# Modulation rows from transposed weights: VectorE multiplies by the conditioning row and sums along it

## The reference, cut to what matters

```python
def adaln(c, w, b):
    mod = jax.nn.silu(c) @ w + b                  # [1, 1024] @ [1024, 3072]
    shift, scale, gate = jnp.split(mod[:, None, :], 3, axis=-1)
    return shift, scale, gate

def modulate(x, norm_w, shift, scale):
    return rmsnorm(x, norm_w) * (1 + scale) + shift
...
# in each sublayer: x = x + gate * sublayer(modulate(x, norm, shift, scale))
```

## Time and profile before

| what | value |
|---|---|
| median of 3 runs | 2490.59 us (2488.46 to 2490.85) |
| profiled execution, its own time | 2491.49 us |
| its span | 2489.7 us |
| mean granted TensorE clock | 0.973 |
| TensorE (PE) busy | 2343.0 us, 94% |
| VectorE (DVE) busy | 1950.8 us, 78% |
| ScalarE (ACT) busy | 1454.8 us, 58% |

### The profile page before, as it was taken

One profiled execution on the slowest core, in us unless ns is written; L12 is line 12 of the kernel. 1 busy time (PEld: TensorE's weight loads), 2 busy tenths in 40 slices (PEclk: granted clock), 3 DMA queues, 4 the chain that ended last, 5 costly groups with the idle time before them and its releaser, 6 DMA issues.

```text
span 2489.7 us, 32549 instructions
## 1 busy us (share of the span) xinstructions
PE 2343.0 (94%) x13701; PEld 2046.0 (82%) x13701; DVE 1950.8 (78%) x2093; ACT 1454.8 (58%) x1665; POOL 249.2 (10%) x303
## 2 busy tenths in 40 slices
PE   5898999899989999999999999997999999899998
PEld 4776998798878888888788888777988997887997
DVE  5857767699669999999898989986667866767875
ACT  3334433367647777777777777765455654446562
POOL 1100111011010000000000000101401211320110
PEclk8998999999989999999999999998999999999999
DMA  9763778464459999999999999975224554213551
GB/s 321 238 209 133 248 261 307 154 248 171 173 208 370 383 372 387 374 386 374 372 369 386 372 383 361 400 294 179 83 96 144 203 203 153 102 68 126 210 206 68
DMA packets 147381, 628.42 MB, mean 252 GB/s; under 512 B 19192, under 2 KB 33882, under 8 KB 125722
## 3 DMA queue, kind: packets, MB, share of 16 engines
q1 hardware_dynamic: 125968, 554.39, 59.6%
q0 software_dynamic: 20176, 71.46, 8.1%
q10 hardware_dynamic: 1082, 0.40, 0.1%
HBM read 615.18 MB, written 11.04 MB: 252 GB/s over the span
## 4 chain that ended last, share of the span: by engine, by line
PE 70%; DVE 17%; DMA 5%; ACT 5%; issue 3%; POOL 1%; SPq 0%; DVEq 0%; ACTq 0%; POOLq 0%
PE ps L134 67%; DVE ul_moe_w L147 3%; PE ps L138 2%; DMA slots<-in_moe_w_gu 2%; DVE macc L155 1%; ACT uh_moe_w L141 1%; DVE eb L147 1%; DVE gate L155 1%; DMA beside<-in_moe_mod_w 1%; DVE ul_ssm_w L147 1%; DMA slots<-in_hyb_mod_w 1%; DVE HT L152 1%; ACT xn L141 1%; DMA beside<-in_dense_mod_w 1%; DVE xn L155 0%
## 5 line engine op out<-in xcount | busy, mean ns | idle before, releaser
L147 DVE TENSOR_TENSOR ul_moe_w<-slots,uh_moe_w 128x2048 fp32r<-128x2048 f32 x334 | 760.7, 2290 | 91.9 <-ACT uh_moe_w L141 90.9
L141 ACT ACTIVATE uh_moe_w<-slots 128x2048 fp32r<-128x2048 f32 x334 | 639.3, 1918 | 181.2 <-PE ps L134 121.3
L134 PE MATMUL ps<-uh_moe_w,XGh 128*128 128x512 f32 x896 | 355.4, 397 | 6.3 <-DVE ul_moe_w L147 4.3
L134 PE MATMUL ps<-uh_moe_w,XGl 128*128 128x512 f32 x896 | 349.5, 390 | 0.0
L134 PE MATMUL ps<-ul_moe_w,XGh 128*128 128x512 f32 x896 | 349.1, 390 | 0.0
L147 DVE TENSOR_TENSOR ul_ffn<-slots,uh_ffn 128x2048 fp32r<-128x2048 f32 x64 | 145.8, 2291 | 79.3 <-ACT uh_ffn L141 79.3
L134 PEld LDWEIGHTS ps<-uh_moe_w,XGh 128*128 128x128 f32 x896 | 168.3, 188 | 45.8 <-DVE ul_moe_w L147 10.3
L134 PE MATMUL ps<-HTf,uh_ffn 128*128 128x256 f32 x704 | 199.5, 283 | 2.0 <-DVE HTlf L147 2.0
L134 PE MATMUL ps<-HTlf,uh_ffn 128*128 128x256 f32 x704 | 199.3, 283 | 0.0
L134 PE MATMUL ps<-HTf,ul_ffn 128*128 128x256 f32 x704 | 199.3, 283 | 0.0
L134 PEld LDWEIGHTS ps<-uh_moe_w,XGl 128*128 128x128 f32 x896 | 168.2, 188 | 36.1
(11 more groups left out here) (557 smaller groups left out, 5450.9 us busy)
## 6 DMA issues: line engine op xcount, KB each, us to landing
slots<-in_moe_w_gu SPq DMA_DIRECT2D x111, 2048.0 KB, 9.7
slots<-in_moe_w_down SPq DMA_DIRECT2D x56, 2048.0 KB, 9.2
slots<-in_w_up SPq DMA_DIRECT2D x20, 2048.0 KB, 8.4
slots<-in_w_in SPq DMA_DIRECT2D x14, 2048.0 KB, 8.8
slots<-in_dense_w_gu SPq DMA_DIRECT2D x10, 2048.0 KB, 11.1
slots<-in_ssm_w_in SPq DMA_DIRECT2D x10, 2048.0 KB, 10.1
slots<-in_w_down SPq DMA_DIRECT2D x10, 2048.0 KB, 7.9
slots<-in_dense_w_down SPq DMA_DIRECT2D x5, 2048.0 KB, 10.6
```

The source lines that it names most:

```text
L134: return self.e.matmul(o, lhsT, rhs, start=start, stop=stop, skip_group_check=skip) if self.e else DONE
L141: return self.e.activation(o, i, f, **kw) if self.e else DONE
L147: return self.e.tensor_tensor(o, a, b, op) if self.e else DONE
```

## The change

The four modulation weights are laid out transposed on the host: part first, then output column, then the 1024 inputs. A chunk is now 128 output columns on the partitions, with 1024 inputs each along the row. silu(c) is spread into a row on all partitions (`scrow`): TensorE multiplies each column of `sc`, broadcast to 128 x 128 as weights, with the identity, and ScalarE copies the two halves out of PSUM. VectorE then multiplies a chunk by `scrow` and sums along the row in one instruction with an accumulator output, which writes one column of `s2`, `s1` or, for a gate, `gcol`. Chunks no longer depend on one another. `column_done` works on the columns in SBUF; a gate's column gets its bias by VectorE, is spread by TensorE like `scrow` and copied by VectorE to `gates[slot]`. The bias DMAs go. Column parts have no empty steps behind them any more, gates two. In the dense stage the pace is (4, 5).

```diff
@@ -154,6 +154,9 @@
...
+    def product_sum(self, o, a, b, total):
+        return self.e.scalar_tensor_tensor(o, a, 1.0, b, ALU.mult, ALU.mult, accum_out=total) if self.e else DONE
     def tensor_copy(self, o, i):
...
@@ -816,7 +819,7 @@
...
     now, later = ("c", "a", "m"), ("b", "g0", "f0", "h0", "g1", "f1", "h1", "ln")
-    sc, sc_e = c.sb("sc", [128, KC]), c.sb("sc_e", [128, KC])
+    sc, sc_e, gcol = c.sb("sc", [128, KC]), c.sb("sc_e", [128, KC]), c.sb("gcol", [128, KC])
     c.ssq, c.rst, c.eps = c.sb("ssq", [128, 2]), c.sb("rst", [128, 2]), c.sb("eps", [128, 1])
...
@@ -825,22 +828,19 @@
...
             s12[f"ln{i}{l}"] = [vec[f"ln{i}_{n}{l}"] for n in ("g", "b")]
-    macc = c.put(12.5, "macc", [128, D])
+    scrow = c.put(12.5, "scrow", [128, D])
     beside = c.put(16.5, "beside", [128, 2, D])
...
     rows.update({b: gates[0][:, i * 128:(i + 1) * 128] for i, b in enumerate(later)})
-    accs = [gates[1], gates[2]]
     ident_landed, x_landed = c.event_signal("ident_landed", 16), c.event_signal("x_landed", 16)
...
     beside_landed = [c.event_signal(f"beside{i}_landed", 16) for i in range(3)]
-    bias_landed = {n: c.event_signal(f"gate_{n}_landed", 16) for n in s12}
     W = io["hyb_mod_w"][0]
-    src = lambda part, k, n: W[k * 128:(k + n) * 128, part * D:(part + 1) * D].rearrange("(a p) n -> p a n", p=128)
+    src = lambda part, k, n: W[part, k * 128:(k + n) * 128, :].rearrange("(a p) n -> p a n", p=128)
     LATE = ((0, 2), (2, 1), (3, 1))
...
@@ -865,7 +865,13 @@
...
         e.activation(sc_e[:, :], vec["c"], AF.Exp, scale=-1.0).then_inc(*S.a.up("exp"))
-        for b in now[1:] + later:
+        rows_of(e, "a")
+        for i in range(2):
+            ps = c.psum.of(("scrow", i))
+            e.wait_ge(*S.t.at(("scrow", i)))
+            e.activation(scrow[:, i * 512:(i + 1) * 512], ps.t[:, :], AF.Copy).then_inc(*S.a.up("scrow"))
+            c.psum.leave(("scrow", i), S.a)
+        for b in now[2:] + later:
             rows_of(e, b)
...
@@ -883,37 +889,35 @@
...
-    def column_sums(e, sig, acc, ready, name, part, pool, ready4=NOTHING):
-        ps = pool.take(("mod", name, part))
-        e.wait_ge(*ps.was)
-        e.wait_ge(*S.g.at("ones"))
-        e.wait_ge(*ready)
-        for i in range(8):
-            if i == 4:
-                e.wait_ge(*ready4)
-            m = e.matmul(ps.t[:, i:i + 1], acc[:, i * 128:(i + 1) * 128], ones[:, 0:1])
-        m.then_inc(*sig.up(("mod", name, part)))
-    def column_done(e, tsig, vsig, name, part):
+    def spread(e, sig, name, ready, cols, pool):
+        for i in range(2):
+            ps = pool.take((*name, i))
+            e.wait_ge(*ps.was)
+            e.wait_ge(*ident_landed.at("ident"))
+            e.wait_ge(*ready)
+            for b in range(4):
+                k = 4 * i + b
+                m = e.matmul(ps.t[:, b * 128:(b + 1) * 128], cols[:, k:k + 1].to_broadcast([128, 128]), K["ident"][:, :])
+            m.then_inc(*sig.up((*name, i)))
+    def column_done(e, sig, name, part):
         s1, s2 = s12[name]
-        ps = c.psum.of(("mod", name, part))
-        e.wait_ge(*tsig.at(("mod", name, part)))
+        s_ = s1 if part else s2
+        e.wait_ge(*sig.now())
         e.wait_ge(*S.v.at(("cols", "m")))
-        s_ = s1 if part else s2
-        e.tensor_tensor(s_[:, :], ps.t[:, 0:8], vec[name + "_mod_b"][:, part * 8:part * 8 + 8], ALU.add).then_inc(*vsig.up(("mod", name, part)))
-        c.psum.leave(("mod", name, part), vsig)
+        e.tensor_tensor(s_[:, :], s_[:, :], vec[name + "_mod_b"][:, part * 8:part * 8 + 8], ALU.add).then_inc(*sig.up(("mod", name, part)))
         if part:
-            e.wait_ge(*vsig.now())
-            e.scalar_tensor_tensor(s1[:, :], s1[:, :], 1.0, vec[name + "_norm"], ALU.add, ALU.mult).then_inc(*vsig.up(("mod", name, "cols")))
+            e.wait_ge(*sig.now())
+            e.scalar_tensor_tensor(s1[:, :], s1[:, :], 1.0, vec[name + "_norm"], ALU.add, ALU.mult).then_inc(*sig.up(("mod", name, "cols")))
     def tensor(e):
-        for b in now:
+        turn(e, "c", c.banks)
+        spread(e, S.t, ("scrow",), S.v.at("sc"), sc, c.banks)
+        for b in now[1:]:
             turn(e, b, c.banks)
-        column_sums(e, S.t, accs[0], S.v.at(("acc", 0)), "hyb", 0, c.banks)
         turn_tensor(c, e, c.hyb, xn, [c.hyb.v.at(("xn", h)) for h in range(2)], (10, 0))
-        column_sums(e, S.t, accs[1], S.v.at(("acc", 1, 0)), "hyb", 1, c.banks, S.v.at(("acc", 1)))
...
@@ -923,15 +927,14 @@
...
         e.tensor_tensor(sc[:, :], sc_e[:, :], vec["c"], ALU.mult).then_inc(*S.v.up("sc"))
-        e.wait_ge(*S.v.now())
+        e.wait_ge(*S.a.at("scrow"))
         for part in range(2):
-            held = NOTHING
             for k in range(8):
...
                             turned(e, b)
-                        column_done(e, S.t, S.v, "hyb", 0)
+                        column_done(e, S.v, "hyb", 0)
                         for h in range(2):
...
@@ -941,21 +944,11 @@
...
                     x = s.t[:, k % 4 * D:(k % 4 + 1) * D]
-                acc = accs[part][:, :]
-                e.wait_ge(*held)
-                if k == 0:
-                    e.tensor_scalar(acc, x, sc[:, 0:1], ALU.mult).then_inc(*S.v.up(("acc", part)))
-                elif part and k == 7:
-                    for i in range(2):
-                        cs = slice(i * 512, (i + 1) * 512)
-                        e.scalar_tensor_tensor(acc[:, cs], x[:, cs], sc[:, k:k + 1], acc[:, cs], ALU.mult, ALU.add).then_inc(*S.v.up(("acc", 1) if i else ("acc", 1, 0)))
-                else:
-                    e.scalar_tensor_tensor(acc, x, sc[:, k:k + 1], acc, ALU.mult, ALU.add).then_inc(*S.v.up(("acc", part)))
-                held = S.v.now()
+                e.product_sum(x, x, scrow[:, :], s12["hyb"][1 - part][:, k:k + 1]).then_inc(*S.v.up())
                 if k % 4 == 3 and not (part and k == 7):
...
         S.v.mark("early")
-        column_done(e, S.t, S.v, "hyb", 1)
+        column_done(e, S.v, "hyb", 1)
...
@@ -968,7 +961,7 @@
...
-        free = [S.t.at(("cols", now[-1])), NOTHING, S.t.at(("mod", "hyb", 1))]
+        free = [S.t.at(("cols", now[-1])), NOTHING, NOTHING]
         for name, slot, bufs, chunks in jobs():
...
@@ -977,7 +970,7 @@
...
                 e.wait_ge(*free[n % 3])
-                e.dma_start(bufs[n % 3], w[k * 128:(k + 1) * 128, part * D:(part + 1) * D]).then_inc(*beside_landed[n % 3].up((name, n)))
+                e.dma_start(bufs[n % 3], w[part, k * 128:(k + 1) * 128, :]).then_inc(*beside_landed[n % 3].up((name, n)))
...
@@ -990,50 +983,43 @@
...
                     if part == 2:
-                        e.wait_ge(*free[2])
-                        if name == "hyb":
-                            e.wait_ge(*S.t.at(("cols", later[-1])))
-                        if name == "dense":
-                            e.wait_ge(*S.t.at(("mod", "hyb", 0)))
-                        e.dma_start(gates[slot][:, :], io[name + "_mod_b"][0, 2 * D:3 * D].partition_broadcast(128)).then_inc(*bias_landed[name].up("bias"))
+                        if name == "ssm":
+                            e.wait_ge(*free[2])
                         yield
-                    yield
-                    yield
+                        yield
                     me.done.add((name, "rows" if part == 2 else ("cols", part)))
...
     def side_vector(e, me):
-        last = NOTHING
+        spread_before = NOTHING
         for name, slot, bufs, chunks in jobs():
+            s1, s2 = s12[name]
             yield
...
                 yield
+                e.wait_ge(*S.a.at("scrow"))
                 e.wait_ge(*beside_landed[n % 3].at((name, n)))
-                if k == 0:
-                    e.wait_ge(*last)
-                    e.tensor_scalar(macc[:, :], bufs[n % 3], sc[:, 0:1], ALU.mult).then_inc(*side.v.up((name, n)))
-                else:
-                    e.wait_ge(*side.v.at((name, n - 1)))
-                    e.scalar_tensor_tensor(macc[:, :], bufs[n % 3], sc[:, k:k + 1], macc[:, :], ALU.mult, ALU.add).then_inc(*side.v.up((name, n)))
+                if part == 2:
+                    e.wait_ge(*spread_before)
+                e.product_sum(bufs[n % 3], bufs[n % 3], scrow[:, :], (s2, s1, gcol)[part][:, k:k + 1]).then_inc(*side.v.up((name, n)))
                 if k < KC - 1:
                     continue
-                if part == 2:
-                    yield
+                if part < 2:
+                    column_done(e, side.v, name, part)
+                    me.done.add((name, ("cols", part)))
+                    continue
+                e.wait_ge(*side.v.now())
+                e.tensor_tensor(gcol[:, :], gcol[:, :], vec[name + "_mod_b"][:, 16:24], ALU.add).then_inc(*side.v.up(("gcol", name)))
                 yield
                 yield
-                if part < 2:
-                    column_done(e, side.t, side.v, name, part)
-                    last = side.t.at(("mod", name, part))
```

(33 more changed lines are left out.)

## The result

The changed kernel took 2453.05 us (median of 4 runs, 2449.78 to 2453.18) against 2490.72 for the kernel before beside it (4 runs): ratio 0.9841, 95% interval 0.9826 to 0.9855, 1.6% faster. The forecast was 2465.0 with a range of 2454 to 2486: the direction was right, the gain of 37.7 us too large for the range. Two further sets of the changed kernel gave 2454.9 and 2454.5 (0.9869 and 0.9855). The profiled execution has a span of 2451.1 against 2489.7.

The account below looks back on a forecast made before the run. TensorE was taken as the bound, waiting for VectorE between its work. Start -2.9, hybrid stage +0.4, dense stage -21 and tail -3.4 gave -27 us from 2491.5, so 2465 us, range 2454 to 2486.

Parts of the forecast that it names:

- The product: VectorE's accumulating product: 1.40 us per chunk, 0.2 of it the accumulator read; four at the start's end give -2.9 us.
- The hybrid stage: Hybrid stage: column sums gone -5.5 us, set against dearer chunks, an extra transfer and gate rows; sum +0.4, bounds -5 and +5.
- The two gate rows' places: Hybrid stage: old row breaking the output projection against new row six steps earlier with a PSUM bank wait; put at 0.
- The lost pause: Hybrid stage: without two empty steps behind each column part, one transfer more on the chain, +2.8 us.
- The dense stage: Dense stage: column sums -9.4, stalls -7.8, slow clock -7, 3 given back; sum -21 us, bounds -25 and -9.
- give-back of 3: Dense stage: 3 us returned because VectorE, at 5.3 of 5.65 us per unit, and its transfers become late next.
- The tail: Dense stage's end: last gate row written earlier, so VectorE's residual follows TensorE; -3.4 us, bounds 0 and -4.
- Everything behind as a block: From the mamba stage's start on: everything moves as one block, with no gain or loss of its own.
- Late transfers as the bound: Rival: VectorE and its transfers bind; dense stage only -9, hybrid stage +3.2, -12 in all, 2479 us; chance 0.22.
- Stalls kept: Rival: the spread waits as the column sum did, twice in the dense stage; -19 in all, 2473 us; chance 0.10.
- Half rate: Rival: VectorE's accumulating product runs at half rate, 2.55 us with the read; +39 in all, 2530 us; chance 0.07.
- nothing: Rival: nothing moves, TensorE's gain is waited for at a weight transfer; 2488 to 2492 us; chance 0.06.

Follow-up runs that it names:

- f4_extra: Changed kernel plus one small VectorE operation (128x8) behind each of the 80 side products that fall behind the start; 2454.6 us.
- h2_hyb: Changed kernel with the two empty steps put back behind the column parts of the dense block's job, which run in the hybrid stage; 2453.8 us.
- e3_pace: Changed kernel with the dense stage's side steps at one per call (1, 1) instead of (4, 5) on TensorE and VectorE; 2469.0 us, ratio 0.9930.
- e2_none: Kernel before with the side column sums left out, the bias row added to itself instead; columns wrong, 2460.55 us.
- g3_late: Changed kernel with four more yields before the expert block's gate row, the last one; 2454.8 us.
- h3_spread: Changed kernel with one empty side step before each of the dense block's chunks 1, 3, 5 and 7; 2454.5 us.
- h4_again: h3_spread run once more, unaltered, in more rounds; 2451.74 us, ratio 0.9842 against the kernel before.

## Why the prediction failed, step by step

**The product.** 1.40 us was mis-sized: it is 1.14. The instruction takes 1.22, not 1.285, and the read of 0.08 us runs beside the next product. The start gained 4.3 instead of 2.9; some 1.0 of the 1.4 us between is the size of four products, the rest that they began 0.5 us earlier. The Trainium skill (VectorE: DVE Perf Modes, section "Two Vector instructions with no wait between them") was right that the accumulating op is two instructions; here the second is hidden. The rule of the Trainium skill on the half rate (Vector Engine (DVE) Microarchitecture Reference, section "Points that are easy to get wrong") did not hold: two float32 sources in SBUF with an accumulator took 1.22 us for 1024 columns, less than the 1.285 of the form without one. That anything but the start profited shows nowhere; f4_extra tests it for a third of the 0.26 us.

**The hybrid stage.** -2.9 and +0.4 were to leave 2.5 us at its end; the profiles of the changed kernel show 2.4, 4.1 and 2.9, and (a) scatters by 4 to 5. The sum is right by luck. The two gate rows' places, set against each other at 0, are not: from 212 to 225 us, where the new row lies, the changed kernel is 3.5 to 5.1 us longer than before, and where the old row lay 2.2 shorter. The lost pause, charged with one transfer of 2.8 us, costs 6.3 to 8.0 (h2_hyb's 238.9 against three profiles), and more than half of that is the gate row's place again and not a transfer.

**The dense stage: the step that failed.** I had -9.4 for the column sums, -7.8 for the stalls, -7 for the clock behind them, and gave back +3 for VectorE and its transfers. The first three are 24.2; with the old code freed of the sums the trace shows 23.5. The two parts were each off and cancel: 17.0 instead of 14.8 for stalls and clock, 6.5 instead of 9.4 for the products. What failed is the give-back of 3. At one step per call it would have been 11.1 us (e3_pace 210.5 against e2_none 199.4), more than three times the price, and in the way of two rivals at once: VectorE late by its transfers, and TensorE waiting for it at the gate rows, with a slow clock behind. At the changed kernel's 4 of 5 it is below nothing, -2.3: the wait of 2.2 us at e2_none's last gate row is gone too. The prediction used the pace to count steps and to work out VectorE's load of 5.3 us in 5.65; it never asked what the slower pace gives. The body gained 25.8 instead of 21.2. (The stage's 218 us were also read from 254.5, where transposes stood; the first dense product starts at 256.81. The sum doesn't use this number.)

**The tail.** -3.4 predicted, 6.6 to 2.9 measured: right. The new row is written at 433 us and the residual does not pass a bias transfer.

**Everything behind as a block: the other step that failed.** Predicted 0. The mamba stage's entry, (c) to (d), fell by 1.7. It did so in e2_none too, where only the column sums are gone, and rose again by 0.5 to 1.1 where the last gate row's products stand behind the last dense product (g3_late, h2_hyb, h3_spread, h4_again); why is not shown. Behind (d) the first profiles differ by 5.0 us in the common code. That is inside the scatter of kernels with that same code, 1394.3 to 1404.1, and below the 5.8 us between two profiles of one kernel (h3_spread, h4_again), but the changed kernel's three profiles stand together at its low end. What part of the 5.0 us belongs to the change stays open. The two spans differ by 38.6 us, 11.7 more than the sum of 26.9. Of these the dense body has 4.6, the entry 1.7, the tail 0.3, start and hybrid stage together none, and 5.0 lie behind (d).

**The rivals.** Late transfers as the bound: true in part of e3_pace, false of the changed kernel. Stalls kept: none kept. Half rate and nothing: refuted. **The range** ended at 2454, where all lower bounds came together, with a give-back of about zero in the dense stage and no gain behind it; three medians, 2453.1 to 2454.9, lie across that end.

## What to carry to other kernels

When work is interleaved by steps, its pace is a term of the sum, not bookkeeping: ask for each consumer how far ahead its producer is when it comes, and what fewer steps per call do to that. An edit that saves steps may pay by the room it makes; the same pace was worth -17.7 us in the old kernel's body and +8 in its total, as the steps did not fit. And an empty step moves all side work behind it: four of them ended the hybrid stage 4 to 10 us earlier, about as much as the new arithmetic gave at the start (4.3) or more, in part by chunks that VectorE need not wait for, in part by the new place of a gate row. Compare such pairs instruction by instruction before naming one cause.

## What the runs showed of the hardware that was not expected

- `DVE_READ_ACCUMULATOR` of one column takes 0.08 us and starts together with the next product: where one product follows another without a wait, it is 1.14 to 1.15 us from start to start, although each is listed with 1.22.
- Stretches of identical instructions differ in length by up to 10 us in 1400 from kernel to kernel, and by 5.8 between two profiles of one kernel. In the 100 us that begin 1160 us behind (c), the granted clock was 0.93 before, 0.97, 0.91 and 0.93 in the three profiles of the changed kernel, 0.93 in h3_spread and 0.97 in h4_again. A gain of a few us at the front of such a kernel can't be read from one total; of the marks above the dense body repeats within 0.1 us in three profiles of one kernel, the hybrid stage's end only within 4 to 5.
- One 4.55 us wait of TensorE was followed by 16 spread products in 3.50 us, where they take 1.9 at the full clock.
